# A decoder layer's mixer as one unrolled plan: inverse and recurrence of neighbouring pairs interleaved, the decode step among z products

## What is computed

```python
proj = rmsnorm(x, norm_mix) @ w_in
qkv  = silu(causal_dwconv(concat(conv_buf, proj[qkv]), w_conv_qkv))
q = l2norm(q) * 128 ** -0.5;  k = l2norm(k)              # 4 heads x 128
log_a = -exp(a_log) * softplus(proj[a] + dt_bias);  beta = sigmoid(proj[b])
# per chunk, g = cumsum(log_a):
a_mat = eye + strict_lower(beta * (k k^T) * exp(g_i - g_j))
u, w  = solve(a_mat, [v * beta, k * beta * exp(g)])
v_new = u - w @ s
o     = (q * exp(g)) @ s + lower((q k^T) * decay) @ v_new
s     = s * exp(g_last) + (k * exp(g_last - g))^T @ v_new
o = rmsnorm(o, w_gdn_norm) * silu(z)
y_sc = proj[B] * causal_dwconv(concat(buf, proj[C] * proj[h]), w_conv_sc)
x = x + concat(o, y_sc) @ w_out
# then x + relu(rmsnorm(x) @ w_up)^2 @ w_down, a gated embedding, a last norm
```

## Time and profile before

| | us |
|---|---|
| runs | 1646.44, 1646.56, 1648.52 |
| median | 1646.56 |
| the profiled execution, its own time | 1649.36 |
| its span, first to last instruction | 1647.8 |
| TensorE busy | 1568.8 (95%) |
| VectorE busy | 726.5 (44%) |
| ScalarE busy | 484.8 (29%) |
| GpSimd busy | 299.2 (18%) |
| mean granted TensorE clock | 0.97 |

### The profile page before, as it was taken

How to read it: one execution, slowest core, us unless ns; L and a number is a source line. 1 busy time by engine, 2 the same in 40 slices (tenths; PEclk the granted TensorE clock), 3 DMA queues, 4 the chain that set the end, 5 groups by cost and what they waited for, 6 DMA issues and landing times.

```text
span 1647.8 us, 26980 instructions
## 1 busy us (share of the span) xinstructions
PE 1568.8 (95%) x9857; PEld 1518.2 (92%) x9857; DVE 726.5 (44%) x1201; ACT 484.8 (29%) x818; POOL 299.2 (18%) x361
## 2 busy tenths in 40 slices
PE   7899899999999858999999999999999999999997
PEld 6899889899999846998999999999999999998997
DVE  5566555454555534225333333333333433335435
ACT  6223322223232241226321303122121313126435
POOL 5100062534526233221000000000000000032213
PEclk9999999999999957999999999999999999999998
DMA  6111110201013033321111111111111111111102
GB/s 165 38 49 40 37 39 14 64 13 52 13 39 105 0 109 93 95 76 39 52 39 51 39 51 49 42 52 39 52 44 47 47 43 52 39 51 55 49 26 106
DMA packets 135718, 86.65 MB, mean 53 GB/s; under 512 B 16507, under 2 KB 130843, under 8 KB 135654
## 3 DMA queue, kind: packets, MB, share of 16 engines
q1 hardware_dynamic: 134502, 81.48, 17.3%
q0 software_dynamic: 1152, 4.33, 0.7%
HBM read 74.58 MB, written 11.21 MB: 52 GB/s over the span
## 4 chain that ended last, share of the span: by engine, by line
PE 85%; DVE 6%; ACT 3%; issue 3%; POOL 1%; DMA 1%; SPq 1%; DVEq 0%; ACTq 0%; POOLq 0%
PE pg L555 64%; PE pg L663 8%; PE bk L703 3%; PE bk L712 2%; DVE act_lo L1656 1%; PE bk L870 1%; PE bk L715 1%; ACT act_hi L972 1%; DVE cv L1416 1%; ACT w_hi L972 1%; POOL XT L1937 1%; DVE qkv L1610 1%; PE bk L682 1%; PE bk L683 0%; DVE w_lo L1335 0%
## 5 line engine op out<-in xcount | busy, mean ns | idle before, releaser
L555 PE MATMUL pg<-act_hi,w_hi 128*128 128x352 f32 x1464 | 480.9, 328 | 17.9 <-issue 4.9
L555 PE MATMUL pg<-act_lo,w_hi 128*128 128x352 f32 x1464 | 473.8, 324 | 0.0
L555 PE MATMUL pg<-act_hi,w_lo 128*128 128x352 f32 x1440 | 464.3, 322 | 0.0
L555 PEld LDWEIGHTS pg<-act_hi,w_hi 128*128 128x128 f32 x1464 | 278.8, 190 | 22.4 <-issue 6.5
L555 PEld LDWEIGHTS pg<-act_lo,w_hi 128*128 128x128 f32 x1464 | 279.1, 191 | 0.0
L555 PEld LDWEIGHTS pg<-act_hi,w_lo 128*128 128x128 f32 x1440 | 272.5, 189 | 0.0
L555 PE MATMUL pg<-u_hi,w_hi 128*128 128x352 f32 x768 | 249.3, 325 | 0.0
L555 PE MATMUL pg<-u_hi,w_lo 128*128 128x352 f32 x768 | 248.9, 324 | 0.0
L555 PE MATMUL pg<-u_lo,w_hi 128*128 128x352 f32 x768 | 247.8, 323 | 0.0
L1991 POOL TENSOR_TENSOR ssq<-ssq,sq 128x352 f32<-128x352 f32 x72 | 77.8, 1094 | 890.2 <-ACT sq L972 889.3
L972 ACT ACTIVATE w_hi<-w_raw 128x1024 fp32r<-128x1024 f32 x111 | 116.7, 1051 | 323.7 <-PE pg L555 301.5
(11 more groups left out here) (295 smaller groups left out, 1845.8 us busy)
## 6 DMA issues: line engine op xcount, KB each, us to landing
w_raw<-in_w_up SPq DMA_DIRECT2D x32, 512.0 KB, 4.0
w_raw<-in_w_down SPq DMA_DIRECT2D x32, 512.0 KB, 3.4
w_raw<-in_w_in SPq DMA_DIRECT2D x29, 512.0 KB, 3.9
x_tok<-in_x_prompt SPq DMA_DIRECT2D x8, 512.0 KB, 7.8
w_raw<-in_w_out SPq DMA_DIRECT2D x8, 512.0 KB, 4.9
x_col<-in_x_prompt SPq DMA_DIRECT2D x8, 512.0 KB, 3.7
w_raw<-in_w_ple_gate SPq DMA_DIRECT2D x8, 512.0 KB, 4.0
out<-y_tok SPq DMA_DIRECT2D x8, 512.0 KB, 2.9
```

What stands on the lines that cost most here:

```text
L555: last = mm(pg[bank][:, 0:TH], w, a, start=i == 0, stop=i == len(terms) - 1)
```

## The change

The mixer's loops are gone: all engines walk through one list, `PLAN`, made by `plan()`. An entry is a step, its chunk and level, and the range of filling behind it; `thirds(a, e)` gives the thirds of units that end in this range, which the other engines then handle in the same place of their queues.

- Units now run in the order k, q, v, z, then C, h, B four times. The eight k and q units come first, by themselves; the filling is 20 units, 1440 matmuls. TensorE does the first third of unit 1 ahead of the last third of the a and b rows (`first_group`), and ScalarE takes the squares of x for the last five token tiles after the high parts. The chain for the decay rates stands in pieces behind the convolutions of units 1 to 4.
- Slot 0 (288 matmuls of filling, the v units): inverse of pair 0.
- Slot 1 (288, the z units): the decode step, its states loaded in slot 0 and stored at the start of slot 2. z gets its SiLU here and is stored.
- Slots 2 to 4 (236 each): inverse of pair s, with the recurrence of pair s - 1 put in, one step after every second step of the inverse. The order of a slot: `vturn` twice, `into`, `kturn`, then `prep` twice, `solve`, `turned` twice, `update`, y, y, `sum`, z, z, `norm`, y, y, `scale`, and so on.
- Last (156): recurrence of pair 3, and the splitting of the mixer output by thirds (`mix`), ahead of the output units.
- k and q are no longer normalised. The sums of squares of k come from the diagonal of k k^T (`accum_out`), and enter through `beta`, the columns of v (`sqk`) and the output's norm, in which the sum of squares of q is added to the sum of squares of o, by one wide matmul (`comb`). g is turned to rows once, written to DRAM and read back spread over the partitions (`load_rows`, `E`). Of the four wide matmuls per chunk one is left.
- Gating is done per chunk (`scale`), z being read back chunk by chunk. The state S and the decode's `S_in` share room: S is zeroed after the sample states are stored.

```diff
+def inverse_steps(s):
+
+    c = (2 * s, 2 * s + 1)
+    steps = [("prep", c[0], 0), ("prep", c[1], 0), ("turned", c[0], 0), ("turned", c[1], 0)]
+    for l in range(1, LEVELS):
+        steps += [("y", c[0], l), ("y", c[1], l), ("z", c[0], l), ("z", c[1], l)]
+    return steps
+
+
+def state_steps(s):
+
+    steps = []
+    for c in (2 * s, 2 * s + 1):
+        steps += [(k, c, 0) for k in ("into", "kturn", "solve", "update", "sum", "norm", "scale")]
+    return steps
+
+
+def plan():
+
+    order = []
+
+    def slot(steps, total):
+        spent = sum(n for _, n in steps)
+        assert total >= spent, (total, spent)
+        last, n = steps[-1]
+        order.extend(steps[:-1] + [(last, n + total - spent)])
+
+    slot([(("begin", 0, 0), 64)] + [(st, {"prep": 14, "turned": 2}.get(st[0], 8)) for st in inverse_steps(0)],
+         9 * KD * NSC)
+    smp = [("s_norm", 16), ("s_conv", 4), ("s_kk", 20), ("s_conv", 4), ("s_xt", 14), ("s_conv", 4), ("s_y", 12),
+           ("s_z", 12), ("s_state", 12), ("s_turn", 10), ("s_solve", 12), ("s_out", 20), ("s_onorm", 14)]
+    count = {}
+    steps = []
+    for k, n in smp:
+        count[k] = count.get(k, -1) + 1
+        steps.append(((k, count[k], 0), n))
+    steps += [(("s_put", i, 0), 8) for i in range(2 * H)]
+    slot([(("s_wait", 0, 0), 6 * KD), (("s_begin", 0, 0), 4)] + steps, 9 * KD * NSC)
+    for s in range(1, NPAIR):
+        steps = [(("vturn", 2 * s - 2, 0), 6), (("vturn", 2 * s - 1, 0), 6)]
+        inv, rec = inverse_steps(s), state_steps(s - 1)
+        steps += [(rec.pop(0), 4), (rec.pop(0), 6)]
+        for i, st in enumerate(inv):
+            steps.append((st, {"prep": 14, "turned": 2}.get(st[0], 6)))
+            if i % 2 == 1 and rec:
+                steps.append((rec.pop(0), 3))
+        assert not rec
+        slot(steps, SLOT_FILL)
+    steps = [(("vturn", NTT - 2, 0), 2), (("vturn", NTT - 1, 0), 2)]
+    steps += [(st, {"scale": 0}.get(st[0], 8)) for st in state_steps(NPAIR - 1)]
+    last = 9 * KD * 3 * NSC - (NPAIR - 1) * SLOT_FILL
+    slot(steps + [(("tail", 0, 0), 0)], last - 6 * KD)
+    order.extend([(("mix", 0, 0), 3 * KD), (("mix", 1, 0), 3 * KD), (("mix", 2, 0), 0)])
+    out, at = [], 0
+    for (k, c, l), n in order:
+        out.append((k, c, l, at, at + n))
+        at += n
+    return out
...
-                    mm(bk[0][:, :], ones[:, :], Tb[0][:, :, :], start=True, stop=True)
-                    mm(bk[1][:, :], ones[:, :], Tb[1][:, :, :], start=True, stop=True)
-                    pe.wait_ge(sm.diag_made, c1)
-                    mm(bk[2][:, :], ones[:, :], X[x][:, :, :], start=True, stop=True) \
-                        .then_inc(sm.norms_summed, 1)
...
+            panel_ready(U_QKV, 0)
+            first_group(0)
             pe.wait_ge(sm.xlo_even, NTT + 1)
             pe.wait_ge(sm.xlo_odd, NTT + 1)
             ab_group(2)
...
+                unit_done(b, 0)
+                if b == 1:
+                    rates()
+                convolve(b)
+                if b == 1:
+                    log1p_start()
+                elif b == 2:
+                    log1p_terms((17, 15, 13, 11))
+                elif b == 3:
+                    log1p_terms((9, 7, 5, 3))
+                elif b == 4:
+                    log1p_end()
+                elif b == U_V - 3:
+                    decays()
+
...
+            def third(b, n):
+                name, i = unit_kind(b)
+                if name == "v":
+                    qkv_third(b, n)
+                    if n == 2:
+                        unit_done(b, 0)
+                        convolve(b)
+                    return
...
+                if k == "begin":
+                    sp.wait_ge(sm.rows_step, 2)
+                    sp.dma_start(g_dram[:, :], LY[1][0:NTT * H, 0, :]).then_inc(sm.rows_out, 16)
+                    sp.wait_ge(sm.rows_out, 16)
+                    load_rows(0)
+                    load_rows(1)
+                    load_in(U_V + 1)
+                    load_in(U_V + 2)
...
+                if k == "prep":
+                    dve.wait_ge(gb_in[x], 16 * (c // 2 + 1))
+                    dve.wait_ge(sm.causal_made, 1)
+                    if c >= 2:
+                        dve.wait_ge(sm.lt_made, lev(c - 2, LEVELS - 1))
+                    for h in range(H):
+                        stt(AT[x][:, h, :], LY[x][:, h, :], g_tok[:, c, h:h + 1], m_inc[:, :], SUB, MIN) \
+                            .then_inc(sm.diff_made, 1)
+                    dve.wait_ge(sm.kk_mm, c + 1)
+                    if c >= 2:
+                        dve.wait_ge(sm.y_mm, lev(c - 2, LEVELS - 1))
+                    for h in range(H):
+                        stt(X[x][:, h, :], A[x][:, h * P:(h + 1) * P], 1.0, ident[:, :], MUL, MUL,
+                            accum_out=ssk[:, c, h:h + 1]).then_inc(sm.diag_made, 1)
+                    dve.wait_ge(sm.diag_made, 4 * (c + 1))
+                    ts_(sbk[:, c, :], ssk[:, c, :], EPS, None, ADD).then_inc(sm.k_step, 1)
+                    dve.wait_ge(sm.k_step, 3 * c + 1)
+                    nc.vector.reciprocal(sbk[:, c, :], sbk[:, c, :]).then_inc(sm.k_step, 1)
+                    dve.wait_ge(sm.k_step, 3 * c + 2)
+                    tt(sbk[:, c, :], sbk[:, c, :], beta[:, c, :], MUL).then_inc(sm.k_step, 1)
+                    dve.wait_ge(sm.kq_mm, c + 1)
+                    dve.wait_ge(sm.decay_made, c + 1)
+                    if c >= 4:
+                        dve.wait_ge(sm.op_mm, c - 3)
+                    tt(PT[s][x][:, :, :], heads(A[2]), AT[x][:, :, :], MUL).then_inc(sm.pt_made, 1)
+                    dve.wait_ge(sm.k_step, 3 * c + 3)
+                    dve.wait_ge(sm.pt_made, c + 1)
+                    for h in range(H):
+                        last = stt(AT[x][:, h, :], A[x][:, h * P:(h + 1) * P], sbk[:, c, h:h + 1], AT[x][:, h, :], MUL, MUL)
+                    last.then_inc(sm.at_made, 1)
+                elif k == "turned":
+                    dve.wait_ge(sm.xt_made, 2 * (c + 1))
+                    nc.vector.transpose(flat(X[x]), flat(XT[s][x])).then_inc(sm.x_copied, 1)
...
+                    if name == "z" and n == 2:
+                        act.wait_ge(sm.evacuated, 12 * b + 12)
+                        op(cv[i % 2][:, 0:T], cv[i % 2][:, 0:T], ACT.Silu).then_inc(sm.z_silu, 1)
+                        log_exp()
```

1794 lines of the change are left out of this document (957 added, 837 removed).

## The result

The changed kernel takes 1627.0 us (median of 4 runs, 1625.9 to 1628.7) against 1646.8 us in the same job: a ratio of 0.988 with an interval of 0.986 to 0.990. It is faster, as forecast, but by 20 us and not by 64, and 1627 lies outside the range of 1560 to 1612.

What follows compares the result with a forecast made beforehand. TensorE was taken as full outside the mixer and nearly full in its loop, but not from 572 to 653. Stage terms summed to 590.5 against 653; with 2.7 for clock, 65.2 us saved: 1584.2, given as 1583, range 1560 to 1612.

Steps and rivals of the forecast that it cites:

- the clock behind the waits of slot 0: Slot 0: stretches at 1.2 GHz that follow TensorE's new waits there were priced at 2.5 us.
- the decode step's own work: Slot 1: the decode step's own TensorE work was put at 20 us, beside 46.3 us of fills.
- the cover of the preparation in slots 2 to 4: Slots 2 to 4: fills would cover VectorE's preparation, its chain ending within 0.2 to 1.3 us of TensorE.
- the queue of SyncE at the start of slot 2: Start of slot 2: only the states' way out, holding the room of the new S, was priced, under 1 us.
- What bounds the kernel, and the norms: Mixer: TensorE nearly full at the earlier trace's unit prices; dropping three of four wide matmuls per chunk saves 20.6 us.
- Start: Before slot 0: early first third of unit 1, decay chain in pieces and clock gain 9.6 us; unit 8 ends at 127.2.
- all four places: Slot 0: new TensorE waits on VectorE, at the load, the preparations and units 10 and 11, sum 19.8 us.
- (c): Slot 0, units 10 and 11: an X update stands behind a convolution, giving waits of 3.6 and 3.5 us.
- (b): Slot 0: unit 9's split and convolution between two preparations make TensorE wait 8.1 us, and GpSimd adds 1.4 us.
- the interleaving leaks: Rival, slots 2 to 4: each of 42 recurrence steps costs 0.6 us, 25 us more, 1608; chance 0.14.
- The table load: Slot 1: a ScalarE table load takes 1283 ns by the row; the skill's 2.66 us would give 1587.
- The slower case: Rival, slots 2 to 4: VectorE stands at recurrence operations, X updates come late, 1.9 us per step gives 1663; chance 0.03.

Runs made afterwards that it cites:

- e9: Changed kernel with the second chunk's four differences of g moved right behind the first chunk's, ahead of its preparation, in each pair: 1612.8 us.
- e1: Changed kernel with the weight loads of units 10 and 11 started ahead of SyncE's wait for the g rows: 1621.3 us.
- e4: Changed kernel with the convolutions of units 9 to 11 taken apart, one operation behind each Y or Z step of slot 0: 1608.0 us.
- e12: Kernel e11 with the decode step's 32 narrow state products set one by one among the fills of slot 1: 1571.4 us.
- e11: Kernel e8 with the edits of e9 and e10 added: 1575.0 us.
- e10: Changed kernel with SyncE loading g rows of chunks 2 and 3 and E ahead of its wait for z's way to DRAM: 1624.5 us.
- e8: Changed kernel with e1, e4, more fills behind preparations, chunk 0's zero-state products and state zeroing left out, and last-slot fills moved behind the sum: 1590.3 us.

## Why the prediction was wrong, step by step

Four terms of the sum failed, and they make up most of the 41.7 us: the clock behind the waits of slot 0 (2.5 us in the forecast, some 10 measured), the decode step's own work (20 us, some 26 measured), the cover of the preparation in slots 2 to 4 (a chain that ends within 1.3 us, 3 to 5 measured), and the queue of SyncE at the start of slot 2 (under 1 us, some 6 measured). The first two had their mechanism right and their size wrong; in the third a duration had been read beside the wrong neighbour, and in the fourth a queue was overlooked.

**What bounds the kernel, and the norms:** right. The prices of the earlier trace rows hold. Slot 3, with a clock of 1.00, took 81.0 us for a forecast of 80.5, the last slot 41.2 for 41. For slot 3 that is partly luck: of the 4.0 us lost in it, 2.8 are the wait on `wn`, which wasn't foreseen, and with 1.1 of them left (e9) the slot took 79.3.

**Start:** 2.9 us short. VectorE now splits the a and b weights 1.1 us later (17.10 instead of 16.01), and this small split, 0.22 us before, takes 1.30, beside a tile of GpSimd:

```profile
17.06 1.27 POOL L2021 TENSOR_TENSOR act_lo<-PT,act_hi 128x512 fp32r<-128x512 f32 x1 [1.75 <-ACT act_hi L1136]
17.10 1.30 DVE L1530 TENSOR_TENSOR w_hi<-w_raw,w_hi 128x64 fp32r<-128x64 f32 x1
```

So TensorE's first products with them wait (`PE pg L688 <- DVE w_hi L1530`, 3.1 us, against 0.4 before) and begin at 18.6 instead of 16.4. I had costed only what the edit gains there. No run tested this place.

**Slot 0:** the mechanism was right at all four places, as e1 and e4 show. The waits came to 24.4 us for 19.8 (with the 1.4 for GpSimd): in (c) I took the split at 1.46 and the convolution at 4.8 from the earlier trace rows, and beside GpSimd's tiles they took 2.2 and 5.9. The sum in (b) has a slip: its four terms give 16.6 and not 16.8. The larger error is the term for the clock, 2.5 us. The slot's work is 73 us at 2.4 GHz, the waits are 24.4, and the slot took 107.6, which is 10.2 more. The four long waits were followed by 3.4, 4.7, 5.8 and 5.2 us at half clock, worth 9.5 us together, and I had counted about one such stretch.

**Slot 1:** the decode step's own work is about 26 us, not 20 (e12: 74.9 less 46.3 of fills less 2.5 of idle time, at a clock of 1.00). I had derived it from busy time multiplied by the mean clock in a stretch that was a third idle, where neither factor is what it seems. It could have been counted: e.g. eight products of 32 rows with 512 columns, at two instructions of 0.53 and 0.52 us, are 8.4 us alone. These 6 us are the whole miss of the slot. A second error didn't show in the changed kernel: the clock, which I took to fall behind waits only, falls behind the narrow products too. It cost 1.7 us there for a forecast of 1.4, which is luck; in e11 it cost 6.4.

**Slots 2 to 4:** here a step failed, the sentence "the preparation's chain ends within 0.2 to 1.3 us of TensorE". It ended 3 to 5 us behind. The preparation's term of 4.6 us adds durations of VectorE read where GpSimd stood still, but the new order puts the second chunk's four differences exactly beside GpSimd's three tiles for the first: 4.1 us instead of 1.1. e9 moves these differences alone, and slots 2 to 4 get 10.7 us shorter. The rival "the interleaving leaks" named 25 us for these slots, where 16.7 were missing, with the wrong mechanism: the leak isn't at each recurrence step, it is at one place in each slot.

**Slot 2:** "the states' way out I put under 1 us" failed. With the zeroing it cost 2.2 us directly, and SyncE's queue, which puts the g rows and `E` behind the last z, another 3.5 (e10). I had walked VectorE's and ScalarE's queues at this place and not SyncE's.

**The total:** 1584.2 less the 2.8 us between the profiled execution and the median is 1581.4, not the 1583 that I gave. Neither is near.

**The table load:** the row and not the 2.66 us that the Trainium skill gives (ScalarE: Activation LUTs, What ACT_TABLE_LOAD costs). ScalarE's load at 144.02 took 1.28 us and the next operation began at 145.31; the wait on ScalarE at the solve was 1.9 us for a forecast of 2.3.

**The slower case** wasn't near: no level of slots 2 to 4 waited over 2 us.

## What to carry to other kernels

When a change interleaves two chains, write for each engine not only how much it has to do between two hand-overs, but what the engine that shares its SBUF access does at that very time. A duration read in the old order is a duration beside the old neighbours. Give each long wait of TensorE a second price for the half clock behind it (here 3.4 to 5.8 us at 1.2 GHz behind each wait of 3.6 us or more in slot 0), and expect a fix to show less in the time than in its stage until the last reason for the clock to fall is gone. Small edits of order (a load ahead of a wait, a long operation in pieces, four operations ahead of GpSimd's, one queue of DMAs, narrow products among wide ones) brought more than twice what the rewrite by itself had brought (56 us in all against 20, e8's omitted products with them).

## What the runs showed of the hardware

- In these traces VectorE's operations with two tiles in SBUF are held up until GpSimd's tile is done: four differences took 4.07 us for 1.13, one on 128x4 elements 0.98 for 0.16. `TENSOR_SCALAR` with one tile in SBUF is held up too (1.80 us for 0.78, 1.31 for 0.17), and so was the start's small split (1.30 us for 0.22). Those with an operand in PSUM were not (0.69 us), nor was the reciprocal (0.18 us at 415.07 in e9).
- TensorE's granted clock fell to 1.2 GHz among or right behind products of 128x8, without a long wait before it (0.8 us was the longest in the 20 us ahead of it), in the changed kernel and in each of e1 to e11, for 3 to 20 us. The length differs between runs in which this part is the same, and I can't say from these runs what sets it.
- Not every wait brings the clock down: the 2.8 us before 425.6 left it at 1.00 in the changed kernel, while e1, with 2.8 us before 421.0 at the same instruction, had 0.50 from 420 to 427. So a stage can differ by 3 to 4 us between kernels that are the same there. How it would come out can't be read from a trace of before.
